# Two projection tiles placed between list products, halved pool clears and an earlier sum of squares, around the first two expert lists of each mixture-of-experts stage

## The chip, the core and the metric

The kernel runs on one core of one Trainium2 chip, as one launch. The metric is device time in microseconds (us), the median of repeated runs of the whole program. All data are 32-bit floats.

## What is computed

One inference step of a decoder with two layers, over 288 tokens (256 of a prompt, 32 of samples) of width 1024. Each layer is a token mixer, then a mixture of experts, then a gated per-layer embedding:

```
for i in range(DEPTH):                       # DEPTH = 2
    hn = _rmsnorm(h, g_mix[i])
    h = h + mixer_i(hn)                      # 0: latent attention, 1: chunked gMLP
    h = h + _hier_moe(_rmsnorm(h, g_ffn[i]), ...)
    h = h + sigmoid(_rmsnorm(h, g_ple[i]) @ w_gate) * (p[i] @ w_proj)
y = _rmsnorm(h, g_final)

def _hier_moe(hn, ...):                      # 32 experts, top 2 of the 8 in the top 1 of 4 groups
    pg = softmax(t @ w_rg + b_rg);  pg_top, g_idx = top_k(pg, 1)
    le_g = (t @ w_re + b_re)[group g_idx];  pe_top, e_idx = top_k(softmax(le_g), 2)
    gates = one_hot(g_idx * 8 + e_idx) * pg_top * pe_top / sum(pe_top)
    a = silu(t @ w_gate) * (t @ w_up) * gates
    return a @ w_down
```

## The kernel before

Tokens lie along the free dimension, features along the 128 partitions, in 8 tiles (KD = 8). All large weights come as one stream of 250 slots of 1 MB through a ring of 12 slots in SBUF. The SP queue issues slot s when slot s - 12 has been released (semaphore `slot_free`): TensorE releases slots with `free_with` on a later matmul, or by a `pe.drain()`. The slots of a layer come in the order in which they are used: one with the projection of the per-layer embedding (`S_PROJ`), 96 with the experts (16 pairs of experts, 6 slots each: four for gate and up, two for down), four for the last gate.

Each engine's program is written out by hand; semaphores tie them together. The change touches the stretch between the last tiles that feed `h` (the output projection of the mixer) and the first expert pair. It runs once per layer, in the function `moe(L)` of each engine:

1. VectorE adds each of the 8 result tiles to `h` (`add_h`, L696), multiplies it by the gain of the norm (`gain`, L700) and adds its squares, which ScalarE made (`sum_sq`, L709). TensorE computes the router's logits of the tile (L1360) and turns the tile into rows of tokens (L1367), both in `route_part`.
2. TensorE sums the squares over the partitions (L1394), ScalarE takes the root (L576), TensorE turns the logits (L1398). ScalarE copies the token rows out of PSUM (L562) and writes them to DRAM (`hn_rows`, L580).
3. VectorE chooses group and experts in a chain of some 30 short instructions (L907 to L929). TensorE meanwhile computes `project(0, 6)`, six of the eight tiles of the embedding's projection (L1411), which ScalarE copies out (L586). ScalarE also computes the exponentials `ex` (L584), which needs a table load.
4. TensorE computes each token's rank in its expert (L1427 to L1432). VectorE builds a 0/1 matrix `member` for a pair of experts (`members`, L954), TensorE multiplies it into a list of token numbers (`list_pair`, L1420), VectorE copies the list out (`take_list`, L962 and L963), and the pool engine gathers the listed rows from DRAM into `x_sel` (`gather`, L352). `x_sel` is cleared before, and so is `y_none`, a block of zeros that is scattered for rows without a token (L341, L342).
5. TensorE turns the gathered rows (`x_turn`, L1448), builds list 3, and begins the first pair: gate and up (L1462), then down (L1471).

Around lists 1 and 2 TensorE runs products of the identity that nothing reads, `keep_busy` (L1151, each one of 128x512): one behind the ranks, one behind `project(6, KD)`, and three behind list 2.

Of the kernel before, what the change touches and what calls it, by code (L numbers as in the profile page):

```python
# [24 lines left out]
D, KD = 1024, 8  # L25
# [59 lines left out]
def program(nc, io, ctx):  # L85
# [251 lines left out]
    def _(pool):  # L337
        def moe(L):

            pool.wait_ge(sem("h_upd"), 8 * (1 if L == 0 else 4))  # L340
            pool.memset(x_sel, 0.0).then_inc(sem("x_clear"), 1)  # L341
            pool.memset(y_none, 0.0).then_inc(sem("x_clear"), 1)  # L342
            pool.wait_ge(sem("hn_rows"), 48 * L + 3 * 16)
            pool.wait_ge(sem("x_clear"), 2 * L + 2)

            def gather(c):

# [55 lines left out]

            for c in range(3):
                gather(c)
            for n in range(PAIRS - 1):
                if n + 3 < PAIRS:
                    gather(n + 3)
                    if n + 3 == PAIRS - 1:
                        scatter_none()  # L410
                scatter(n)
# [44 lines left out]
    def _(act):  # L456
# [97 lines left out]
        def moe(L):  # L554
# [24 lines left out]
            for t, (t0, tn) in enumerate(TOK):  # L579
                act.dma_start(hn_rows[L][t0:t0 + tn, :], hn_tok[0:tn, t, :]).then_inc(sem("hn_rows"), 16)  # L580
            for m in range(KD):
                if m == 5:
                    act.wait_ge(sem("sel"), 2 * L + 2)
                    nc.scalar.activation(ex, dx, ACT.Exp).then_inc(sem("ex"), 1)  # L584
                act.wait_ge(sem("prj_ps"), 8 * L + m + 1)
                nc.scalar.activation(prj[:, m, :], bank(2 + m % 4, T), ACT.Copy).then_inc(sem("prj"), 1)  # L586
# [83 lines left out]
    def _(dve):  # L670
# [213 lines left out]
        for m in range(KD):  # L884
            dve.wait_ge(sem("h_part"), m + 1)
            add_h(m, bank(m % 4, T))
            dve.wait_ge(sem("h_upd"), m + 1)
            gain("ffn0", m, hn_t, G_FFN[0])
            if m >= 1:
                sum_sq("ffn0", m - 1)  # L890
        sum_sq("ffn0", KD - 1)

        io3 = const[:, C_IOTA:C_IOTA + EPG]

# [235 lines left out]
        for m in range(KD):  # L1130
            dve.wait_ge(sem("h_part"), 16 + m + 1)
            add_h(m, bank((m + 1) % 4, T))
            dve.wait_ge(sem("h_upd"), 24 + m + 1)
            gain("ffn1", m, hn_t, G_FFN[1])
            if m >= 1:
                sum_sq("ffn1", m - 1)
        sum_sq("ffn1", KD - 1)
        dve.wait_ge(sem("out"), 64)
        moe(1)
        for k in range(0, KD, 2):  # L1140
# [4 lines left out]
    def _(pe):  # L1145
# [207 lines left out]
            last.then_inc(sem("o_ps"), 1)  # L1353
        owe(1)
        pe.wait_ge(sem("o_sb"), H)
        def route_part(L, k):

            pe.wait_ge(sem("scales"), 2)
            pe.wait_ge(sem("h_upd"), 8 * H_STAGE[f"ffn{L}"] + k + 1)
            last = mm(ps[0:G + NE, 7, 0:T], w_r[:, L, k, :], h_t[:, k, :], start=(k == 0), stop=(k == KD - 1))  # L1360
            if k == KD - 1:
                last.then_inc(sem("lg_ps"), 1)
            pe.wait_ge(sem("h_gain"), 8 * H_STAGE[f"ffn{L}"] + k + 1)
            if k == 4:
                pe.wait_ge(sem("hr_a"), 6 * L + 3)
            for t, (t0, tn) in enumerate(TOK):
                last = nc.tensor.transpose(ps[0:tn, 4 + t, (k % 4) * P:(k % 4) * P + P], hn_t[:, k, t0:t0 + tn], ident)  # L1367
            if k % 4 == 3:
                last.then_inc(sem("hr_ps"), 1)

        for m in range(KD):
            if m % 2 == 0:
                wait_slots(pe, S_O + m // 2, S_O + m // 2 + 1)
            if m >= 4:
                pe.wait_ge(sem("h_upd"), m - 3)
            for k in range(H):
                last = mm(bank(m % 4, T), ring(S_O, m * D + k * P, P), oT[:, k, :], start=(k == 0), stop=(k == H - 1))  # L1377
                if k == 0:
                    free_with(last)
            last.then_inc(sem("h_part"), 1)  # L1380
            if m % 2 == 1:
                owe(1)
            if m >= 2:
                route_part(0, m - 2)

        def moe(L):
            ffn = f"ffn{L}"
            route_part(L, KD - 2)
            route_part(L, KD - 1)

            pe.wait_ge(sem("scales"), 5 + 2 * L)
            pe.wait_ge(sem("h_sum"), 8 * H_STAGE[ffn] + KD)
            for t in range(3):
                last = mm(ps[:, 0, t:t + 1], sq_sum[:, t * P:t * P + P], ones[:, 0:1], start=True, stop=True)  # L1394
            last.then_inc(sem("h_ss"), 1)
            pe.wait_ge(sem("lgs"), L + 1)
            for t in range(3):
                last = nc.tensor.transpose(ps[:, 1, 36 * t:36 * t + 36], lgs[:, t * P:t * P + P], ident[0:G + NE, 0:G + NE])  # L1398
# [33 lines left out]
                last = mm(ps[:, 6, 0:32], ones[0:tn, :], sel[0:tn, t, :], start=(t == 0), stop=(t == 2))  # L1432
            last.then_inc(sem("rank_ps"), 1)
            keep_busy(0, 1)
            project(6, KD)
            keep_busy(0, 1)
            pe.drain().then_inc(sem("slot_free"), 1)

            pe.wait_ge(sem("tv"), 2 * (L + 1))
            list_pair(1, None)  # L1440
            list_pair(2, 1)
            keep_busy(0, 3)
            pe.wait_ge(sem("prj"), 8 * L + KD)

            def x_turn(b):
# [226 lines left out]
        for m in range(KD):  # L1672
            if m >= 4:
                pe.wait_ge(sem("h_upd"), 24 + m - 3)
            last, at = out_part(m, OUT_K if m < 4 else 0, FT, at)
            last.then_inc(sem("h_part"), 1)
            if m >= 2:
                route_part(1, m - 2)
        moe(1)
        sum_norm("fin")  # L1680

# [131 lines left out]
```

## Time and profile before

| | |
|---|---|
| median of 3 runs | 1193.99 us (1192.52 to 1194.03) |
| profiled execution | 1194.44 us |
| its span in the trace | 1192.7 us |
| TensorE busy | 1065.9 us (89%) |
| VectorE, ScalarE, pool busy | 369.3, 189.9, 115.0 us |
| DMA | 306.02 MB, mean 257 GB/s |

In the rows a PE row is TensorE's matmuls (a matmul of 32-bit floats is two records), PEld its weight loads, DVE is VectorE, ACT ScalarE, POOL the pool engine, and SPq, ACTq the sequencers of SP and ScalarE. Times count from the start of the span. PEclk is the clock granted to TensorE as a share of its 2.4 GHz: 1.00 is that level, 0.50 is 1.2 GHz, and a share between them says how much of the stretch was at each.

### The profile page before, as it was taken

How to read it: one execution, taken by the hardware profiler on the slowest of the kernel's cores; microseconds unless marked ns; L12 is line 12 of the kernel's file. 1: busy time of each engine (PE TensorE's matmuls, PEld its weight loads, DVE VectorE, ACT ScalarE, POOL GpSimd, SP SyncE). 2: the span in 40 equal slices, each digit the busy share in tenths (PEclk: the TensorE clock that was granted, in tenths of full speed). 3: DMA queues.
4: the chain of work that ended last, by engine and by line, in shares of the span. 5: the costliest groups of instructions: out<-in, count | busy, mean ns of one | idle time of the engine just before them, and what ended most of it. 6: DMA issues, size and time to landing. Idle time of an engine off the chain costs nothing.

```text
span 1192.7 us, 14363 instructions
## 1 busy us (share of the span) xinstructions
PE 1065.9 (89%) x5248; PEld 656.7 (55%) x5248; DVE 369.3 (31%) x929; ACT 189.9 (16%) x389; POOL 115.0 (10%) x152
## 2 busy tenths in 40 slices
PE   6978699999988886999999999999999998787693
PEld 5747366544433332777777777777644443332272
DVE  4545214322221101562227444221422221110164
ACT  2122112211111101231112110001211111011121
POOL 1333000111111111000000000000111111110101
PEclk9989799899999999999999999999979999999897
DMA  9758282499999996933333323333269999999501
GB/s 367 301 166 257 74 359 108 150 397 421 417 420 419 419 420 256 421 144 138 115 132 141 106 106 106 106 132 138 98 245 411 419 418 418 419 420 382 223 33 40
DMA packets 62613, 306.02 MB, mean 257 GB/s; under 512 B 13746, under 2 KB 23186, under 8 KB 30546
## 3 DMA queue, kind: packets, MB, share of 16 engines
q1 hardware_dynamic: 45936, 275.73, 58.3%
q0 software_dynamic: 13632, 22.58, 5.7%
q10 hardware_dynamic: 2978, 6.80, 1.5%
q8 instruction: 44, 0.72, 0.2%
q14 instruction: 23, 0.19, 0.0%
HBM read 308.10 MB, written 21.08 MB: 276 GB/s over the span
## 4 chain that ended last, share of the span: by engine, by line
PE 64%; DMA 23%; issue 5%; DVE 3%; SPq 3%; ACT 1%; POOL 0%; POOLq 0%; DVEq 0%; ACTq 0%
DMA ring_sb<-stream 23%; PE ps L1607 16%; PE ps L1462 10%; PE ps L1655 8%; PE ps L1471 4%; PE ps L1540 3%; PE ps L1377 3%; PE ps L1160 2%; PE ps L1420 2%; PE ps L1151 2%; PE ps L1202 1%; SPq L292 1%; SPq L293 1%; PE ps L1558 1%; PE ps L1556 1%
## 5 line engine op out<-in xcount | busy, mean ns | idle before, releaser
L1462 PE MATMUL ps<-ring_sb,scr_sb 128*64 128x512 f32 x1024 | 236.4, 609 | 41.0 <-DMA ring_sb<-stream 41.0
L1607 PE MATMUL ps<-hn_sb,ring_sb 128*128 128x288 f32 x768 | 194.9, 408 | 0.0
L1462 PEld LDWEIGHTS ps<-ring_sb,scr_sb 128*64 128x64 f32 x1024 | 78.7, 140 | 194.6 <-issue 194.5
L1607 PEld LDWEIGHTS ps<-hn_sb,ring_sb 128*128 128x128 f32 x768 | 142.6, 190 | 37.3 <-DVE hn_sb L700 0.3
L1471 PE MATMUL ps<-ring_sb,scr_sb 128*64 128x512 f32 x512 | 121.4, 617 | 2.1 <-ACT scr_sb L598 1.9
L986 DVE SCALAR_TENSOR_TENSOR scr_sb<-ps,scr_sb 128x256 f32<-128x256 f32 x32 | 15.5, 483 | 267.0 <-ACT scr_sb L594 267.0
L1655 PE MATMUL ps<-scr_sb,ring_sb 128*128 128x288 f32 x384 | 95.3, 407 | 0.0
L1655 PEld LDWEIGHTS ps<-scr_sb,ring_sb 128*128 128x128 f32 x384 | 72.2, 190 | 19.4
L1471 PEld LDWEIGHTS ps<-ring_sb,scr_sb 128*64 128x64 f32 x512 | 34.9, 141 | 61.7 <-issue 57.4
L1540 PE MATMUL ps<-scr_sb,ring_sb 128*128 128x288 f32 x256 | 64.3, 406 | 0.0
L352 POOL DMA_INDIRECT scr_sb<-hn_rows,scr_sb x32 | 32.4, 1014 | 301.5 <-DVE scr_sb L963 276.7
L1077 DVE TENSOR_TENSOR scr_sb<-ps,rstd_sb 128x288 f32<-128x288 f32 x48 | 21.7, 453 | 124.4 <-PE ps L1607 120.8
L1540 PEld LDWEIGHTS ps<-scr_sb,ring_sb 128*128 128x128 f32 x256 | 48.6, 190 | 13.4
L594 ACT ACTIVATE scr_sb<-ps,scr_sb 128x256 f32<-128x256 f32 x32 | 15.2, 474 | 239.7 <-PE ps L1462 239.7
L991 DVE TENSOR_SCALAR scr_sb<-ps,scr_sb 128x512 f32<-128x512 f32 x32 | 24.0, 751 | 93.0 <-PE ps L1471 89.5
L1420 PEld LDWEIGHTS ps<-tv_sb,scr_sb 128*128 128x128 f32 x384 | 48.2, 202 | 4.6 <-DVE scr_sb L954 2.5
L1420 PE MATMUL ps<-tv_sb,scr_sb 128*128 128x4 f32 x384 | 48.0, 254 | 2.8 <-DVE scr_sb L954 2.4
L696 DVE TENSOR_TENSOR h_sb<-h_sb,ps 128x288 f32<-128x288 f32 x32 | 14.4, 451 | 111.8 <-PE ps L1655 54.0
L341 POOL MEMSET scr_sb<- 128x2048 f32 x2 | 3.6, 1803 | 469.4 <-DVE h_sb L696 469.4
L471 ACT ACTIVATE scr_sb<-h_sb 128x288 f32<-128x288 f32 x48 | 21.1, 439 | 173.5 <-DVE h_sb L696 173.5
L602 ACT ACTIVATE scr_sb<-ps,scr_sb 128x512 f32<-128x512 f32 x32 | 22.0, 687 | 144.5 <-PE ps L1471 140.0
L369 POOL DMA_INDIRECT y_rows<-scr_sb x30 | 29.8, 993 | 144.4 <-DVE scr_sb L991 141.0
(258 smaller groups left out, 1098.6 us busy)
## 6 DMA issues: line engine op xcount, KB each, us to landing
ring_sb<-stream SPq DMA_DIRECT2D x249, 1024.0 KB, 18.3
scr_sb<-key_pages SPq DMA_DIRECT2D x64, 192.0 KB, 3.4
ring_sb<-row_pages POOLq DMA_DIRECT2D x64, 128.0 KB, 3.5
scr_sb<-y_rows POOLq DMA_DIRECT2D x8, 512.0 KB, 5.0
hn_rows<-scr_sb ACTq DMA_DIRECT2D x4, 512.0 KB, 3.1
h_sb<-x SPq DMA_DIRECT2D x1, 1152.0 KB, 5.6
scr_sb<-bs ACTq DMA_DIRECT2D x1, 640.0 KB, 12.9
scr_sb<-p ACTq DMA_DIRECT2D x2, 288.0 KB, 5.2
```

Source lines behind the costliest of these rows:

```text
L352: pool.indirect_dma_start(out=x_sel[:, c % 2, :], out_offset=None, in_=hn_rows[L], in_offset=bass.IndirectOffsetOnAxis(ap=slots[:, c, 0:1] ...
L369: pool.indirect_dma_start(out=y_rows[L], out_offset=bass.IndirectOffsetOnAxis(ap=slots[:, c, 1:2], axis=0), in_=y_sb[:, c % 2, :], in_offs ...
L991: nc.vector.tensor_scalar(y_sb[:, b, 512:1024], bank(6), g[:, 0:1], None, ALU.mult).then_inc(sem(f"y_sb{L}"), 1)
L1151: mm(bank(b), ident, const[:, 0:512], start=True, stop=True)
L1160: last = mm(bank(m, T), ring(S_IN, m * D + k * P, P), hn_t[:, k, :], start=(k == 0), stop=(k == KD - 1))
L1377: last = mm(bank(m % 4, T), ring(S_O, m * D + k * P, P), oT[:, k, :], start=(k == 0), stop=(k == H - 1))
L1420: last = mm(ps[:, 7, 0:4], member[:, q, :], tv[:, q // 3, q % 3, :], start=(q == 0), stop=(q == 5))
L1462: last = mm(ps[64 * a:64 * a + 64, 2 + b, :], xT[:, k, 64 * a:64 * a + 64], slot(a + 2 * (k // 4))[:, (k % 4) * 512:(k % 4) * 512 + 512], ...
L1471: last = mm(ps[64 * a:64 * a + 64, 5 + n, :], aT[:, k, 64 * a:64 * a + 64], slot(4 + k)[:, a * D + n * 512:a * D + n * 512 + 512], start=( ...
L1540: last = mm(bank(PLE_BANK[m % 4], T), ring(s, (m % 2) * D + k * P, P), hgp[:, k, :], start=(k == 0), stop=(k == KD - 1))
L1607: last = mm(bank((i + 1) % 4, T), ring(s, (i % 2) * D + k * P, P), hn_t[:, k, :], start=(k == 0), stop=(k == KD - 1))
L1655: last = mm(bank((m + 1) % 4, T), ring(s, (at % 16) * P, P), uT[:, k, :], start=(k == 0), stop=(k == FT - 1))
```

## The change

In `moe(L)` of TensorE, `route_part` is split into `logits` and `turn_rows`, and the last tile's `turn_rows` goes behind the sum of the squares. On VectorE the last `gain` goes behind the last `sum_sq`. The pool engine clears `x_sel` in two halves, the first when all squares are summed, the second when the first member matrix is there, and `y_none` behind the third gather. ScalarE loads the table of Exp ahead of the fourth projection copy, by a one-column activation. Of the last two projection tiles the seventh goes behind list 1 and the eighth behind list 2; four of the five `keep_busy` products of this stretch are taken out, and the `pe.drain()` that releases the slot of the projection moves behind the eighth tile.

```
             pool.wait_ge(sem("h_upd"), 8 * (1 if L == 0 else 4))        # before
             pool.memset(x_sel, 0.0).then_inc(sem("x_clear"), 1)
             pool.memset(y_none, 0.0).then_inc(sem("x_clear"), 1)
             pool.wait_ge(sem("hn_rows"), 48 * L + 3 * 16)
             pool.wait_ge(sem("x_clear"), 2 * L + 2)
...
             pool.wait_ge(sem("h_sum"), 8 * H_STAGE[f"ffn{L}"] + KD)     # the change
             pool.memset(x_sel[:, 0, :], 0.0).then_inc(sem("x_clear"), 1)
             pool.wait_ge(sem("hn_rows"), 48 * L + 3 * 16)
             pool.wait_ge(sem(f"member{L}"), 2)
             pool.memset(x_sel[:, 1, :], 0.0).then_inc(sem("x_clear"), 1)
             pool.wait_ge(sem("x_clear"), 3 * L + 2)
```

```diff
@@ pool engine, behind the first three gathers
+            pool.memset(y_none, 0.0).then_inc(sem("x_clear"), 1)
+            pool.wait_ge(sem("x_clear"), 3 * L + 3)
@@ ScalarE
             for m in range(KD):
+                if m == 3:
+                    nc.scalar.activation(eps[:, 2:3], eps[:, 0:1], ACT.Exp)
                 if m == 5:
@@ VectorE (the same for ffn1)
-            gain("ffn0", m, hn_t, G_FFN[0])
+            if m < KD - 1:
+                gain("ffn0", m, hn_t, G_FFN[0])
             if m >= 1:
                 sum_sq("ffn0", m - 1)
         sum_sq("ffn0", KD - 1)
+        gain("ffn0", KD - 1, hn_t, G_FFN[0])
@@ TensorE, moe(L)
-            route_part(L, KD - 2)
-            route_part(L, KD - 1)
+            logits(L, KD - 2)
+            turn_rows(L, KD - 2)
+            logits(L, KD - 1)
...
             last.then_inc(sem("h_ss"), 1)
+            turn_rows(L, KD - 1)
             pe.wait_ge(sem("lgs"), L + 1)
...
             keep_busy(0, 1)
-            project(6, KD)
-            keep_busy(0, 1)
-            pe.drain().then_inc(sem("slot_free"), 1)
 
             pe.wait_ge(sem("tv"), 2 * (L + 1))
             list_pair(1, None)
+            project(6, 7)
             list_pair(2, 1)
-            keep_busy(0, 3)
+            project(7, KD)
+            pe.drain().then_inc(sem("slot_free"), 1)
             pe.wait_ge(sem("prj"), 8 * L + KD)
```

TensorE's order behind the ranks of layer 0, before: L1151 is `keep_busy`, L1411 `project`, L1420 `list_pair` (its second stretch of six is list 2), L1448 `x_turn`, L1462 the first pair's gate and up.

```order
L1432 MATMUL ps<-scr_sb,const_sb 128x32 x3
L1151 MATMUL ps<-const_sb 128x512
L1411 MATMUL ps<-scr_sb,ring_sb 128x288 x4
L1151 MATMUL ps<-const_sb 128x512
L1420 MATMUL ps<-tv_sb,scr_sb 128x4 x12
L1151 MATMUL ps<-const_sb 128x512 x3
L1448 MATMUL ps<-const_sb,scr_sb 128x128 x8
L1420 MATMUL ps<-tv_sb,scr_sb 128x4 x6
L1462 MATMUL ps<-ring_sb,scr_sb 64x512 x16
```

The same place in the change, whose lines are L1446 for the ranks, L1160 `keep_busy`, L1434 `list_pair`, L1425 `project`, L1461 `x_turn`, L1475 gate and up:

```order
L1446 MATMUL ps<-scr_sb,const_sb 128x32 x3
L1160 MATMUL ps<-const_sb 128x512
L1434 MATMUL ps<-tv_sb,scr_sb 128x4 x6
L1425 MATMUL ps<-scr_sb,ring_sb 128x288 x2
L1434 MATMUL ps<-tv_sb,scr_sb 128x4 x6
L1425 MATMUL ps<-scr_sb,ring_sb 128x288 x2
L1461 MATMUL ps<-const_sb,scr_sb 128x128 x8
L1434 MATMUL ps<-tv_sb,scr_sb 128x4 x6
L1475 MATMUL ps<-ring_sb,scr_sb 64x512 x16
```

List 1 now stands directly behind one filler product, each list is followed by one tile (two matmuls) of projection, and no filler stands between list 2 and the turn of the gathered rows.

The pool engine's order at the head of its `moe(0)`, before (the semaphores that it waits for in brackets):

```order
L341 MEMSET scr_sb 128x2048 [waits h_upd]
L342 MEMSET scr_sb 128x1024
L352 DMA scr_sb<-hn_rows,scr_sb 128x1024 [waits slots0,hn_rows,x_clear]
L352 DMA scr_sb<-hn_rows,scr_sb 128x1024 [waits slots0]
L352 DMA scr_sb<-hn_rows,scr_sb 128x1024 [waits slots0,x_ps0] x2
```

and in the change (L353 is the gather there):

```order
L341 MEMSET scr_sb 128x1024 [waits h_sum]
L344 MEMSET scr_sb 128x1024 [waits member0,hn_rows]
L353 DMA scr_sb<-hn_rows,scr_sb 128x1024 [waits x_clear,slots0]
L353 DMA scr_sb<-hn_rows,scr_sb 128x1024 [waits slots0]
L353 DMA scr_sb<-hn_rows,scr_sb 128x1024 [waits slots0,x_ps0]
L407 MEMSET scr_sb 128x1024
```

The clear of 2048 columns has become two of 1024 with waits of their own, and the clear of `y_none` stands behind the third gather.

## Rows read from the trace of the kernel before

**Rows 1.** Waits of PE in the expert stage of layer 0 (total, times, longest).

```profile
PE ps L1462 <- DMA ring_sb<-stream: 19.2, 16, 2.3
```

**Rows 2.** Stretches (PE, PEld, DVE, ACT, POOL busy; PEclk, DMA share, GB/s).

```profile
241.00:246.00 5.00, 5.00 (x22) 1.60 (x20) 0.75 (x1) 0.69 (x1) 0.55 (x1) 0.85 0.95 345
251.00:256.00 5.00, 4.79 (x32) 3.08 (x32) 2.37 (x6) 1.45 (x3) 0.52 (x1) 1.00 1.02 418
```

**Rows 3.** The chain in order of time, layer 0 (start, us, what).

```profile
202.92 0.80 PE ps L1394 x6
...
204.03 6.02 PE ps L1411 x24
...
211.71 1.05 PE ps L1151 x2
212.76 1.94 PE ps L1411 x8
...
215.79 1.49 PE ps L1420 x12
...
218.45 2.62 PE ps L1420 x12
221.07 4.90 PE ps L1151 x6
225.98 0.88 PE ps L1448 x8
226.85 1.24 PE ps L1420 x12
228.09 7.04 PE ps L1462 x32
```

**Rows 4.** Timeline of layer 0 (start, us, engine, line, operands, [idle before <-releaser]).

```profile
199.93 1.99 DVE L700 TENSOR_SCALAR hn_sb<-h_sb,par_sb 128x288 f32<-128x288 f32 x1
199.95 1.81 POOL L341 MEMSET scr_sb<- 128x2048 f32 x1 [90.15 <-DVE h_sb L696]
...
201.43 0.68 PE L1360 MATMUL ps<-h_sb,w_r_sb 128*36 128x288 f32 x2
201.69 1.11 POOL L342 MEMSET scr_sb<- 128x1024 f32 x1
...
204.33 0.27 DVE L910 TENSOR_TENSOR scr_sb<-ps,scr_sb 128x108 f32<-128x108 f32 x1
...
209.54 1.28 ACT L584 ACT_TABLE_LOAD   x1
...
211.08 0.17 DVE L935 TENSOR_REDUCE scr_sb<-scr_sb 128x3 f32<-128x12 f32 x1 [0.51 <-ACT scr_sb L584]
...
213.34 0.96 DVE L954 TENSOR_TENSOR scr_sb<-const_sb,scr_sb 128x768 f32<-128x768 f32 x1
...
218.56 1.07 POOL L352 DMA_INDIRECT scr_sb<-hn_rows,scr_sb  x1 [15.75 <-issue]
```

**Rows 5.** Line L700 over the span: durations min/median/max in ns, first and last start.

```profile
L700 DVE TENSOR_SCALAR hn_sb<-h_sb,par_sb x32: 369/370/1994, 167.3 to 1175.1; 128x288 f32<-128x288 f32 x32
```

**Rows 6.** Line L352 in the stretch 218 to 220: its DMA.

```profile
DMA to landing us min/median/max: 3.2/3.2/3.2
```

**Rows 7.** Stretches around the changes of PEclk, columns as in rows 2.

```profile
218.00:219.00 1.00, 0.55 (x3) 0.55 (x4) 0.57 (x2) 0.00 (x0) 0.44 (x1) 0.80 1.00 426
...
225.00:226.00 1.00, 1.00 (x4) 0.37 (x3) 0.00 (x0) 0.00 (x0) 0.00 (x0) 0.79 0.02 4
...
242.00:243.00 1.00, 1.00 (x6) 0.34 (x4) 0.00 (x0) 0.00 (x0) 0.00 (x0) 0.76 0.99 418
...
888.00:891.00 3.00, 3.00 (x8) 0.71 (x6) 0.00 (x0) 0.00 (x0) 0.00 (x0) 0.50 0.68 277
```

**Rows 8.** The chain in order of time: down products of the first pairs.

```profile
239.42 5.12 PE ps L1471 x16
...
885.21 5.31 PE ps L1471 x11
```

More of the change, by code:

```diff
@@ L338, in moe @@
         def moe(L):
-            pool.wait_ge(sem("h_upd"), 8 * (1 if L == 0 else 4))
-            pool.memset(x_sel, 0.0).then_inc(sem("x_clear"), 1)
-            pool.memset(y_none, 0.0).then_inc(sem("x_clear"), 1)
+            pool.wait_ge(sem("h_sum"), 8 * H_STAGE[f"ffn{L}"] + KD)
+            pool.memset(x_sel[:, 0, :], 0.0).then_inc(sem("x_clear"), 1)
             pool.wait_ge(sem("hn_rows"), 48 * L + 3 * 16)
-            pool.wait_ge(sem("x_clear"), 2 * L + 2)
+            pool.wait_ge(sem(f"member{L}"), 2)
+            pool.memset(x_sel[:, 1, :], 0.0).then_inc(sem("x_clear"), 1)
+            pool.wait_ge(sem("x_clear"), 3 * L + 2)
             def gather(c):
@@ L1133, in _ @@
             dve.wait_ge(sem("h_upd"), 24 + m + 1)
-            gain("ffn1", m, hn_t, G_FFN[1])
+            if m < KD - 1:
+                gain("ffn1", m, hn_t, G_FFN[1])
             if m >= 1:
@@ L1137, in _ @@
         sum_sq("ffn1", KD - 1)
+        gain("ffn1", KD - 1, hn_t, G_FFN[1])
         dve.wait_ge(sem("out"), 64)
@@ L1355, in _, with logits @@
         pe.wait_ge(sem("o_sb"), H)
-        def route_part(L, k):
+        def logits(L, k):
             pe.wait_ge(sem("scales"), 2)
@@ L1362, in route_part, with turn_rows @@
                 last.then_inc(sem("lg_ps"), 1)
+        def turn_rows(L, k):
             pe.wait_ge(sem("h_gain"), 8 * H_STAGE[f"ffn{L}"] + k + 1)
@@ L1383, in _ @@
             if m >= 2:
-                route_part(0, m - 2)
+                logits(0, m - 2)
+                turn_rows(0, m - 2)
         def moe(L):
             ffn = f"ffn{L}"
-            route_part(L, KD - 2)
-            route_part(L, KD - 1)
+            logits(L, KD - 2)
+            turn_rows(L, KD - 2)
+            logits(L, KD - 1)
             pe.wait_ge(sem("scales"), 5 + 2 * L)
@@ L1677, in _ @@
             if m >= 2:
-                route_part(1, m - 2)
+                logits(1, m - 2)
+                turn_rows(1, m - 2)
         moe(1)
```

## The prediction

> **What bounds the kernel now.** I read first who waits for whom in the expert stage, then the stretches of that stage, then the chain in order of time ahead of it, then the timeline there with the granted clock. In the expert stage of layer 0 TensorE waits 16 times for the weight stream, 19.2 us in all [rows 1], and from about 251 us the stream moves 418 GB/s with the DMA share at 1.00 [rows 2]. So that stage ends when the stream has brought its last slot. But the stream can only refill what TensorE has released: at 241 to 246 it still moved 345 GB/s [rows 2], because the first pair's slots were coming free too slowly. From there on nothing slackens. A microsecond by which TensorE works off the first pair earlier or later is therefore a microsecond of the stage's end, in each layer; what happens elsewhere inside the stage is not. The mark to watch is the end of the first gate and up product, 228.09 + 7.04 = 235.13 us [rows 3].
>
> Ahead of it the chain is TensorE's [rows 3]: sum of squares, projection, ranks, a filler to 212.76, two projection tiles, a filler, list 1 at 215.79, list 2 at 218.45, three fillers from 221.07, 4.90 us, the turned rows at 225.98, list 3 at 226.85. The fillers are the obvious waste. The first gather was issued at 218.56 [rows 4] and landed 3.2 us later, at 221.8 [rows 6]: the rows lay there for 4.2 us before they were turned.
>
> **The start of the chain.** The last gain took 1.99 us on VectorE beside a clear of 1.81 us on the pool engine [rows 4], where 370 ns is the median of its line [rows 5]: it was held until the clear was done, and both sums of squares behind it with it. With the sums first, they end about 1.9 us sooner. TensorE can't use all of that: it computes the last logits until 201.43 + 0.68 = 202.11 [rows 4], so its sum over partitions starts there and not at 202.92 [rows 3], 0.8 us sooner. Behind it now stands the turn of the last tile (three transposes, 0.5 us by the spacing of that stretch), so the turned logits, and with them VectorE's chain, come about 0.55 us sooner than 204.33 [rows 4]. The first half clear now starts together with the last gain and may hold it for its 1.11 us (a clear of 1024 columns [rows 4]); the gain then ends near 202.2, while TensorE is at the sum: hidden, and 0.5 us at most if it isn't.
>
> The Trainium skill ("SBUF — State Buffer", Who interferes with whom) says that VectorE in its two-port form and the pool engine block each other for a whole instruction, by order of issue. The 1.99 us agree. By it the half clear could also be the one that is held, for 0.4 us, which nobody waits for; the sum is the same.
>
> **The exponentials.** Their table load stood at 209.54 and VectorE waited 0.51 us for them [rows 4]. It now stands ahead of the fourth copy. ScalarE still has its three row writes and five copies to do before the exponentials, so it arrives near 210.05; VectorE, 0.55 us sooner, is there at 209.99 and waits 0.3. That gives 0.2 us more (between 0 and 0.51). The first member matrix, which was done near 213.34 + 0.96 = 214.30 [rows 4], is done at 214.30 - 0.55 - 0.2, some 213.55.
>
> **The lists.** TensorE is through with ranks and one filler 0.3 us sooner, at 212.45, and waits for the matrix. List 1 starts at 213.6, not 215.79: 2.2 us won. It takes 1.49 us [rows 3].
>
> **The clock.** This decides what is left of it. The granted clock was 1.00 until 218.6 (a share of 0.80 in 218 to 219) and 0.50 until 225.4 (0.79 in 225 to 226) [rows 7], that is 1.2 GHz. It fell 3.0 us after the last filler ahead of list 1 ended, with nothing but list 1 and a wait between. In this low stretch list 2 took 2.62 us, where list 3 took 1.24; three fillers took 4.90 us, where one took 1.05 at the high level; the clock came back 4.35 us after these fillers had begun [rows 3, 7]. In the change the unbroken work ends at 212.45 and what follows up to gate and up is lists, waits and two tiles of 0.97 us each (two tiles took 1.94 [rows 3]). I see nothing there that would keep the clock high or bring it back, so I take it as low from somewhere in list 1 until 4.35 us after gate and up has begun. The sum, from 213.6:
>
> - list 1: between 1.49 and 2.62, taken 1.9: to 215.5
> - seventh tile: between 0.97 and 1.94, taken 1.5; it covers VectorE's 1.17 us for the next member matrix (218.45 less 215.79 + 1.49): to 217.0
> - list 2, low: 2.62, to 219.6
> - eighth tile, low: 1.94, to 221.55, and ScalarE's copy with its two handovers, which TensorE waits for, taken 0.6 (no group shows it waited for; the same handovers cost VectorE's list 0.2 to 0.3 and a copy of this size cannot be under the 0.37 of a VectorE gain, so 0.5 to 0.8), to 222.15. The first gather, issued 1.3 us behind list 1's end and landing 3.2 us later, is there by 220 and is not waited for
> - turned rows, low: twice 0.88, to 223.9
> - list 3, low: 2.62, to 226.5
>
> So gate and up begins 1.6 us sooner. But it starts at half clock: of its first 4.35 us half is lost, 2.2 us. It ends at 226.5 + 7.04 + 2.2 = 235.75 against 235.13: 0.6 us later. The fillers' 4.90 us bought the clock, and the change pays for it inside the products that count. The clock fell once more in both layers behind the first gate and up, and I leave that as it is: it is an idle stretch that the change doesn't touch.
>
> **What costs nothing.** The slot of the projection is released near 221.5, not at 215.6: it fetches slot 23, down weights of the second pair, with the ring otherwise full. The cover is the whole first pair; without it, one slot would cost 2.5 us (1.05 MB at 418 GB/s [rows 2]). The second half clear, 1.11 us, runs while TensorE makes list 1 (1.49), and is past before the list is out; if not, the gather comes late by up to 1.1 us and still lands before the eighth tile is copied. The clear of `y_none`, 1.11 us, falls into the first gate and up and may hold VectorE's small operations for row numbers; the product lasts 7 us. SP and ScalarE's DMAs are as many as before; ScalarE's three row writes come 0.5 us sooner.
>
> **The sum.** 0.6 us in each of two layers is 1.2 us. The profiled execution took 1194.44 us, 0.45 over the median of 1193.99; applied to the median, the forecast is 1195.2 us, a change within what can be told from none. Faster or slower by 0.2%, 2.4 us, is what a measurement of this kernel can tell.
>
> **Rivals.**
>
> - Main case, 1193 to 1197.5: chance 0.46.
> - The clock holds all the way. Then only the gather binds: landed at 219.6, turned by 220.5, list 3 by 221.7, where it was 228.09: 6.4 us in each layer, 1181.2 us. Against it: the clock fell with less idling than the change leaves. Chance 0.08.
> - The clock is low for the lists, but the eighth tile and the turned rows, 3.7 us of low-clock work with 0.6 us of waiting in them, bring it back by the start of gate and up. Then the 2.2 us are not lost: 1.6 us won per layer, 1190.8 us. For it: list 2 and three fillers, also work at the low level, did end with the clock back [rows 3, 7]. Chance 0.16.
> - It comes out slower: the clock is low from the start of list 1, which adds 0.7 + 0.4 us to my middle values, and comes back late. In layer 1 the down products that began at 885.21 [rows 8] still ran at 0.50 up to 891 [rows 7], 5.8 us, while in layer 0 those of 239.42 had it back at 242.5, 3.1 us [rows 7, 8]. With 5.8 for 4.35 another 0.7 us is lost: 0.6 + 1.8 = 2.4 us per layer, 1198.8 us. It decides from 1.2 us per layer. Chance 0.20.
> - The change doesn't do what it says, since the stream hides the start of the stage: 1194.0 us. The 345 GB/s [rows 2] speak against it. Chance 0.10.
>
> The Trainium skill ("TensorE: Matmul & The Clock Gate", Part 4) says that transposes don't count like products for the clock. By it the third case falls away, since half of its work is turned rows, and the forecast stays 1195.2; if they did count it would be 1190.8. No row here separates the two, so I keep the chance.
>
> **How the numbers follow.** The range must reach from the third case to the fourth; 1188 leaves room for a shorter low stretch in one layer, 1199 for the long one in both. The case of the held clock, 0.08, is left out, and some 0.05 beyond the upper end. Faster by over 0.2%: 0.08, two thirds of 0.16, and a little of the main case, 0.20. Slower: most of the fourth case and an eighth of the main case, 0.28. The rest, 0.52, is no change.
>
> **What would show it.** List 1 starting 2.2 us sooner, near 213.6; the last gain no longer ahead of the sums; PEclk at 0.50 in the turned rows and for some 4 us of gate and up; gate and up beginning near 226.5 and ending near 235.7. The forecast is wrong if PEclk is 1.00 there, or if the stream at 241 to 246 moves much more or less than 345 GB/s for another reason.

## The result and the profile after

The changed kernel took 1184.86 us (median of 5, 1180.24 to 1185.20), the kernel before beside it 1192.60 us: a ratio of 0.9922, 95% interval 0.9902 to 0.9941, so 0.6 to 1.0% faster. The forecast was 1195.2 in a range of 1188 to 1199. Both the time and the range were wrong. The profiled execution took 1184.96 us, its span is 1183.3 us against 1192.7.

Where the 9.4 us of span lie is read by setting marks of the two traces against each other: the end of the last h update ahead of the expert stage, the start of the first gate and up product, the end of the stage's last down product, and the first product that combines the rows behind it (L1556 before, L1569 after).

| stretch | before | after | difference |
|---|---|---|---|
| start to last h update, layer 0 | 199.89 | 199.18 | -0.7 |
| h update to first gate and up, layer 0 | 28.13 | 26.56 | -1.6 |
| h update to last down product, layer 0 | 268.94 | 268.91 | 0.0 |
| last down product to first combining one, layer 0 ("exit") | 9.84 | 10.68 | +0.8 |
| from there to the last h update, layer 1 | 366.89 | 367.28 | +0.4 |
| h update to first gate and up, layer 1 | 27.92 | 24.18 | -3.7 |
| h update to last down product, layer 1 | 272.69 | 268.59 | -4.1 |
| exit of layer 1 | 11.37 | 5.11 | -6.3 |
| from there to the end | 63.13 | 63.53 | +0.4 |

(All in us; each row on the first gate and up product is part of the row below it.) Layer 0 is much as forecast. Layer 1 isn't, and the largest single difference lies behind the stage, in a stretch that the prediction doesn't mention.

The chain in order of time of the changed kernel, layer 0, which answers to [rows 3] (L917 the start of VectorE's chain, L961 the member matrix, L1434 the lists, L1425 a projection tile, L591 its copy, L1461 turned rows, L1475 gate and up):

```profile
202.94 0.28 DVE scr_sb L917
...
211.36 0.97 DVE scr_sb L961
212.47 1.91 PE ps L1434 x12
214.38 2.13 PE ps L1425 x4
216.50 2.35 PE ps L1434 x12
218.86 2.14 PE ps L1425 x4
221.02 0.42 ACT scr_sb L591
221.49 1.97 PE ps L1461 x8
223.46 2.35 PE ps L1434 x12
225.81 9.34 PE ps L1475 x32
```

and the same view in layer 1:

```profile
859.33 1.49 PE ps L1434 x12
...
861.99 2.72 PE ps L1434 x12
864.70 2.14 PE ps L1425 x4
866.87 0.42 ACT scr_sb L591
867.33 1.73 PE ps L1461 x8
869.07 1.24 PE ps L1434 x12
870.30 7.04 PE ps L1475 x32
```

One kernel, two outcomes. In layer 0 gate and up takes 9.34 us, in layer 1 7.04. The stretches, columns as in [rows 2], say why:

```profile
214.00:230.00 16.00, 15.50 (x52) 10.78 (x54) 7.36 (x24) 1.42 (x3) 4.04 (x4) 0.50 0.46 159
241.00:246.00 5.00, 5.00 (x26) 1.71 (x24) 0.75 (x1) 0.69 (x1) 1.46 (x2) 1.00 1.00 393
862.00:868.50 6.50, 6.00 (x22) 4.89 (x23) 1.65 (x7) 0.74 (x2) 2.02 (x2) 0.50 0.17 39
869.00:877.00 8.00, 8.00 (x45) 3.42 (x43) 4.69 (x14) 0.60 (x1) 1.95 (x2) 1.00 0.83 307
```

In layer 0 the granted clock was 0.50, that is 1.2 GHz, until 230, 4.6 us into gate and up. In layer 1 it was 1.00 from the end of the turned rows on, with no idle-time product behind list 1. The first is the prediction's main case, the second its third rival. The clock also didn't fall a second time in layer 0: at 241 to 246 it was 1.00, and the stream moved 393 GB/s, where the kernel before had 0.85 and 345 GB/s [rows 2].

Now the exit. The chain behind the last down product, kernel before, layer 0 and then layer 1 (L1471 down, L1151 three products of 512 columns that fill time; "issue" is time in which the engine waited for nothing that the profile shows):

```profile
465.18 3.65 PE ps L1471 x16
468.83 5.21 issue
474.04 4.79 PE ps L1151 x6
...
1114.60 3.65 PE ps L1471 x16
1118.25 6.09 issue
1124.35 5.49 PE ps L1151 x6
```

The same of the changed kernel from the end of the down products on (L1160 the fillers):

```profile
468.10 1.48 issue
469.58 0.70 PE ps L1160
470.27 4.28 issue
474.55 4.43 PE ps L1160 x5
...
1114.64 1.24 issue
1115.88 2.41 PE ps L1160 x5
1118.29 0.92 issue
1119.21 0.70 PE ps L1160
```

Between the last down product and these fillers TensorE reads how many tokens the fullest expert has and jumps over the code for further passes. Before, it stood still for 5.21 and 6.09 us there. After, it goes on within 1.24 to 1.48 us, but stops again among the fillers: behind one record of six in layer 0, behind five of six in layer 1. The change touches nothing in this place. A stop that moves by a few instructions when code far ahead is taken out points at the fetching of instructions. The DMA view has a queue for it, and in the stretch of the stop of the kernel before, layer 1 (1114.5 to 1124.3 us), it shows one transfer:

```profile
q8 instruction: 1, 0.02, 0.9%
```

Over the span it is (changed kernel):

```profile
PE 1061.7 (90%) x5232; PEld 656.7 (55%) x5232; DVE 370.4 (31%) x929; ACT 189.9 (16%) x391; POOL 115.0 (10%) x154
q8 instruction: 44, 0.72, 0.2%
```

44 transfers of 16 KB. They come every 10 to 37 us wherever TensorE runs straight on, with one more at each of the two exits. With 5232 records of matmuls that is one transfer for 119 records, or about 60 products of the code.

### The profile page after: what moved, and what is told of

Its sections match the earlier page's. It is cut to its first block, busy times and chain, and to the rows that moved or that the text cites. A ratio compares the mean times of both kernels' runs of the same rounds, so it can differ in the third digit from the quotient of the medians.

```text
span 1183.3 us, 14338 instructions
## 1 busy us (share of the span) xinstructions
PE 1061.7 (90%) x5232; PEld 656.7 (55%) x5232; DVE 370.4 (31%) x929; ACT 189.9 (16%) x391; POOL 115.0 (10%) x154
## 4 chain that ended last, share of the span: by engine, by line
PE 63%; DMA 24%; issue 4%; DVE 4%; SPq 3%; ACT 1%; POOL 0%; POOLq 0%; DVEq 0%; ACTq 0%
DMA ring_sb<-stream 23%; PE ps L1620 16%; PE ps L1475 11%; PE ps L1668 8%; PE ps L1484 4%; PE ps L1553 3%; PE ps L1388 3%; PE ps L1169 2%; PE ps L1434 2%; PE ps L1211 1%; SPq L292 1%; SPq L293 1%; PE ps L1569 1%; PE ps L1571 1%; PE ps L1643 1%
## 5 line engine op out<-in xcount | busy, mean ns | idle before, releaser
L1475 PE MATMUL ps<-ring_sb,scr_sb 128*64 128x512 f32 x1024 | 240.9, 618 | 41.2 <-DMA ring_sb<-stream 41.2
L1475 PEld LDWEIGHTS ps<-ring_sb,scr_sb 128*64 128x64 f32 x1024 | 80.0, 141 | 197.3 <-issue 197.3
L353 POOL DMA_INDIRECT scr_sb<-hn_rows,scr_sb x32 | 32.5, 1014 | 274.8 <-DVE scr_sb L970 251.1
L1553 PEld LDWEIGHTS ps<-scr_sb,ring_sb 128*128 128x128 f32 x256 | 48.6, 190 | 13.4
L1434 PEld LDWEIGHTS ps<-tv_sb,scr_sb 128*128 128x128 f32 x384 | 49.7, 206 | 4.6 <-issue 3.8
L1434 PE MATMUL ps<-tv_sb,scr_sb 128*128 128x4 f32 x384 | 49.0, 257 | 2.3 <-DVE scr_sb L961 2.2
L1461 PEld LDWEIGHTS ps<-const_sb,scr_sb 128*128 128x128 f32 x256 | 28.8, 146 | 27.1 <-issue 24.5
```

What stands on the lines that cost most here:

```text
L353: pool.indirect_dma_start(out=x_sel[:, c % 2, :], out_offset=None, in_=hn_rows[L], in_offset=bass.IndirectOffsetOnAxis(ap=slots[:, c, 0:1] ...
L1434: last = mm(ps[:, 7, 0:4], member[:, q, :], tv[:, q // 3, q % 3, :], start=(q == 0), stop=(q == 5))
L1461: last = nc.tensor.transpose(ps[:, k // 4, (k % 4) * P:(k % 4) * P + P], x_sel[:, b, k * P:(k + 1) * P], ident)
L1475: last = mm(ps[64 * a:64 * a + 64, 2 + b, :], xT[:, k, 64 * a:64 * a + 64], slot(a + 2 * (k // 4))[:, (k % 4) * 512:(k % 4) * 512 + 512], ...
L1553: last = mm(bank(PLE_BANK[m % 4], T), ring(s, (m % 2) * D + k * P, P), hgp[:, k, :], start=(k == 0), stop=(k == KD - 1))
```

## The experiments

"Narrow product" below is this. It moves all code behind it and does little work. It isn't quite free: in layer 0's first pairs, where TensorE hardly waits, two of them for each pair make a pair take 14.04 us and not 13.36 (e6); later the wait for the stream hides them:

```
def one_column(b, n):
    for _ in range(n):
        mm(ps[:, b, 0:1], ident, const[:, 0:1], start=True, stop=True)
```

All results first, from 4 to 12 runs each; exits are read as above from each run's one profiled execution. The kernel before was run along with each group of four: 1193.98, 1194.01, 1194.07 and 1192.85 us.

| run | median us (range) | ratio to before, 95% | exit 0 | exit 1 |
|---|---|---|---|---|
| e1 after, 4 narrow per layer | 1195.93 (1194.2 to 1199.1) | 1.0023 (1.0010, 1.0036) | 9.29 | 9.53 |
| e2 after, 4 of 512 columns per layer | 1193.17 (1190.7 to 1197.9) | 1.0000 (0.9984, 1.0016) | 8.92 | 10.30 |
| e3 before without four fillers | 1187.28 (1184.4 to 1188.7) | 0.9949 (0.9929, 0.9969) | 9.77 | 4.87 |
| e4 before, the four narrowed | 1192.93 (1191.1 to 1196.2) | 0.9996 (0.9982, 1.0010) | 10.03 | 9.63 |
| e5 after, shift by 16 | 1182.00 (1176.0 to 1186.5) | 0.9896 (0.9864, 0.9929) | 5.75 | 3.99 |
| e6 after, shift by 32 | 1180.05 (1178.0 to 1181.2) | 0.9871 (0.9847, 0.9895) | 4.13 | 6.22 |
| e7 after, shift by 48 | 1181.36 (1178.2 to 1185.7) | 0.9870 (0.9840, 0.9899) | 4.16 | 3.89 |
| e8 after, shift by 64 | 1186.26 (1181.3 to 1191.5) | 0.9936 (0.9913, 0.9958) | 8.71 | 5.12 |
| e9 before, shift by 32 | 1183.51 (1182.7 to 1186.0) | 0.9913 (0.9900, 0.9926) | 4.14 | 3.91 |
| e10 lists alone, shift by 32 | 1186.53 (1181.2 to 1190.1) | 0.9932 (0.9911, 0.9954) | 4.14 | 5.93 |
| e11 start alone, shift by 32 | 1180.95 (1178.3 to 1188.7) | 0.9909 (0.9883, 0.9935) | 4.23 | 4.43 |
| e12 as e6 | 1181.43 (1179.9 to 1182.2) | 0.9896 (0.9881, 0.9910) | 4.85 | 4.63 |
| e13 before, no jump | 1183.41 (1181.7 to 1187.3) | 0.9919 (0.9897, 0.9941) | 4.35 | 4.42 |
| e14 after, no jump | 1181.37 (1176.4 to 1185.6) | 0.9886 (0.9857, 0.9915) | 3.73 | 3.54 |
| e15 after, shift by 1 | 1187.09 (1182.6 to 1191.2) | 0.9948 (0.9930, 0.9967) | 8.84 | 5.73 |
| e16 e2, shift by 32 | 1184.10 (1181.1 to 1187.4) | 0.9913 (0.9890, 0.9937) | 4.77 | 3.90 |

**Is it the work or the place of the code? (e1 to e4)** e1 and e2 add to the changed kernel, ahead of the turned rows:

```diff
             pe.drain().then_inc(sem("slot_free"), 1)
+            one_column(0, 4)      # e2: keep_busy(0, 4)
             pe.wait_ge(sem("prj"), 8 * L + KD)
```

e1:

> The changed kernel, with four products of one column per layer where the three idle-time products stood, ahead of the turned rows of the first pair, so that TensorE has as many instructions as in the kernel before, at a cost of some 0.1 us each that the wait for ScalarE's last copy hides. Theory A (the 6 us come from behind the last down product, and depend on where TensorE's instructions lie behind the skipped branch): the time from the last down product to the first combining product goes back to about 9.8 us in layer 0 and 11.4 us in layer 1, 1190 us in all. Theory B (they come from the new order and timing of the lists): it stays at 10.7 and 5.1 us, 1185 us in all.

e2:

> The changed kernel, with four products of 512 columns per layer at that place. Theory A: the exits as in the run with narrow products, and beside that what the products do to the clock and to the first turned rows (up to 1 us a layer either way), 1188 to 1192 us. Theory B, the products cost what the change saved: also about 1190 us, but with exits of 10.7 and 5.1 us and a list stage that is later by 2 to 3 us in each layer.

e3 and e4 leave the kernel before as it is but for its four fillers:

```diff
             project(6, KD)
-            keep_busy(0, 1)
+            # e4: one_column(0, 1)
             pe.drain().then_inc(sem("slot_free"), 1)
...
-            keep_busy(0, 3)
+            # e4: one_column(0, 3)
```

e3:

> The kernel before without four of its five products of 512 columns per layer (the one ahead of the slots' release and the three ahead of the turned rows), all else as it was. Theory A: the exits take about 10.7 and 5.1 us, so 1187 to 1188 us, with the list stages no faster. Theory B: the exits stay at 9.8 and 11.4 us, 1192 to 1195 us.

e4:

> The kernel before with the same four products narrowed to one column. Theory A: exits as in the kernel before, 9.8 and 11.4 us, so 1192 to 1194 us. Theory B: 1192 to 1195 us too. Beside the run without them it shows what the count of instructions is worth where the work is the same.

With eight products of one column more, 16 records, the changed kernel takes 11 us more. Its exits are 9.29 and 9.53 us, 3.0 us longer together. The chain of e1, layer 0:

```profile
470.39 4.94 issue
475.33 4.51 PE ps L1160 x6
```

The stop comes at once, ahead of all six records, as in the kernel before, in e2 and in e4, which have as many products ahead of the jump. Most of the rest of e1's loss is in layer 1's stage, 274.72 us against 268.59: its clock was low to 878, and I come to that below. Part of it is the four products themselves. I had expected 0.1 us each, hidden; at the low clock the four took 1.9 us, and list 3 came 3.6 us behind the eighth tile and not 2.3. The kernel before without four fillers per layer (e3) has exits of 9.77 and 4.87 us, with one record ahead of the stop in layer 0 and five in layer 1, exactly as in the changed kernel, though its lists are the old ones; it gains 6.7 us. Its chain in layer 1 up to the sixth record:

```profile
1118.11 1.27 issue
1119.38 2.41 PE ps L1151 x5
1121.79 0.65 issue
```

With the four narrowed (e4) the gain is gone, 5.7 us in the median and 5.0 us in the exits, which are 10.03 and 9.63 us. Theory A stands; B, that the lists bring the 6 us, fell. The misses: I expected 1190 us for e1, and it took 1195.9, because I left layer 1's clock and the products' own time out of it. For e2 I expected 1188 to 1192, and it took 1193.2. And where the stop comes at once it isn't always as long as the 11.4 us of exit that I expected in layer 1: e1, e2 and e4 had 9.5 to 10.3 there.

**Does it follow the transfers? (e5 to e8)** 1, 2, 3 and 4 narrow products ahead of each of the 16 pairs' gate and up in layer 0:

```diff
                 pe.wait_ge(sem(f"xT{L}"), 2 * (n + 1))
+                one_column(2 + b, 1 if L == 0 else 0)      # 2, 3, 4
                 for k in range(KD):
```

> The changed kernel with one product of one column ahead of each pair's gate and up products in layer 0, 16 in all, about a quarter of the code that one 16 KB transfer of instructions holds (44 transfers for 5232 recorded matmuls, two records to a product, so about 60 products to a transfer). The products lie in stages that wait for the weight stream. Theory C (what matters is where the code behind the skipped branch lies in those transfers): as in the run with four narrow products per layer, the code behind the branch is not there when TensorE jumps, exits of 9 to 10 us in both layers, 1190 to 1196 us. Rival D (any more instructions cost some time everywhere): a little over 1185 us, exits of 10.7 and 5.1 us.

> The same with two such products for each pair of layer 0, 32 in all, about half a transfer. Theory C: either as with a quarter, or, if by now the branch and what lies behind the skipped code are in transfers that follow one another, exits of 4.5 to 5.5 us in both layers and 1179 to 1181 us. Rival D: 1185 to 1187 us, exits of 10.7 and 5.1 us.

> The same with three such products for each pair of layer 0, 48 in all, about three quarters of a transfer. Theory C: the code behind the branch is there when TensorE jumps, with a good part of its transfer left: exits of 4.5 to 5.5 us in both layers, 1179 to 1181 us. Rival D: 1185 to 1188 us.

> The same with four such products for each pair of layer 0, 64 in all, about one whole transfer. Theory C: the place in the transfers is nearly that of the changed kernel, so its exits come back, near 10.7 and 5.1 us or one product to the side of them, 1181 to 1190 us. Rival D: 1186 to 1190 us, and no such swing between the four runs.

More instructions made the kernel faster: 1180 to 1182 us with 16, 32 and 48 of them, and slower again at 64, 1186 us. (At 16 the interval of the ratio still overlaps that of the changed kernel; the exits are short.) With 64 the pattern of the changed kernel is back, one record and then the stop (e8, layer 0):

```profile
469.29 1.45 issue
470.75 0.70 PE ps L1160
471.44 2.33 issue
473.78 4.43 PE ps L1160 x5
```

Rival D fell by this return: a price per instruction rises, it doesn't come back to the same picture after 64 products, about what one transfer holds. What is left of it is the time of the products themselves, as above. For a quarter I had expected the long exits, and it had short ones: the stretch of places in which the code is missing is the narrower part of the period here, not the wider. In the short exits TensorE goes on in one piece (e5, layer 1):

```profile
1106.76 1.31 issue
1108.07 2.84 PE ps L1160 x6
```

and in layer 0 of e5 the combining product then waits another 1.24 us for the rows that the pool engine loads back. That wait is the floor of an exit: the 6.22 us in layer 1 of e6 and the 5.93 us in layer 1 of e10 are it too.

The traces tie the stops to the transfers more closely. In all 16 exits with a stop (both layers of before, after, e1 to e4, e8 and e15) a transfer of 16 KB begins on q8 behind the last down product, and TensorE goes on 1.3 to 1.6 us behind its end, whether the stop is 0.7 or 6.2 us long. The transfer before it lay 21 to 27 us ahead of the end of the last down product. In the 16 exits that have the jump and no stop (e5 to e7, e9 to e12, e16) it lay 0.8 to 19 us ahead, which fits code around the jump that had been fetched more lately.

**How sharp is the border? (e15)** A single narrow product, at the first pair of layer 0.

> The changed kernel with one single product of one column more, in layer 0 ahead of the first pair's gate and up products. Theory A with a sharp border: in layer 0, where one record of an idle-time product ran ahead of the stop, none is left and the stop comes at once, 9 to 10 us of exit; in layer 1, where five records ran ahead of it, three are left and the stop is longer by about their time, 5 to 6 us of exit: 1184 to 1187 us. Rival, no sharp border: exits as in the changed kernel, 10.7 and 5.1 us.

The chain of e15, layer 0 and layer 1:

```profile
467.43 4.46 issue
471.89 4.54 PE ps L1160 x6
...
1112.27 1.28 issue
1113.55 1.55 PE ps L1160 x3
1115.10 1.50 issue
1116.61 1.55 PE ps L1160 x3
```

As expected to the record: one product of two records moved the stop from behind one record to ahead of all, and in layer 1 from behind five to behind three. The exits, 8.84 and 5.73 us, are a little under the 9 to 10 and within the 5 to 6 expected; the median, 1187.09, is just above the 1184 to 1187.

**Is it the jump? (e13, e14)** TensorE's code for further passes left out (these inputs never run it), for a kernel that doesn't jump:

```diff
-            with pe.If(most > WIN):
-                with pe.Fori(PAIRS // 2, PASSES * PAIRS // 2) as i:
...
```

> The kernel before with TensorE's code of the further passes left out (they run only if an expert has more tokens than one window, which these inputs don't have), so that TensorE jumps over nothing; the other engines keep theirs. Theory A, in the form that the jump over code costs a transfer that isn't there: exits of 4 to 6 us in both layers, about 1182 us. Rival, the place in the transfers costs it without a jump too: exits of 8 us or more in one layer at least, 1186 us or more.

> The changed kernel with the same code left out of TensorE's part. Theory A: exits of 4 to 6 us, about 1180 us, and not further from the kernel before without it than 1 to 4 us: the change's own worth once more. Rival as there.

The kernel before goes from 1192.9 to 1183.4 us. Its timeline in layer 1:

```profile
1113.86 2.83 PE L1151 MATMUL ps<-const_sb 128*128 128x512 f32 x6 [0.83 <-issue]
1117.45 0.86 PE L1535 MATMUL ps<-const_sb,scr_sb 128*128 128x128 f32 x6 [0.75 <-DMA scr_sb<-y_rows]
```

and its transfers of instructions:

```profile
q8 instruction: 42, 0.69, 0.2%
```

Two fewer than 44: the ones at the exits are gone, and the wait is for the loaded rows. So both are needed for the stop, the jump and an unlucky place behind it. The Trainium skill says just that ("Runtime: NRT & Kernel Launch", Instruction fetch mechanics): a taken branch whose target isn't among the pages that are held forces a fetch before execution goes on. These runs agree. From the last down product to the first filler it is 4.4 to 6.2 us of "issue" where the code is missing altogether (before, e1, e2, e4, layer 0 of e15), against 1.2 to 1.7 us with a jump to code that is held and 0.8 to 1.1 us without a jump (e13, e14).

**What is the change itself worth? (e9 to e12, e16)** All with 32 narrow products, and no exit in their traces stops. e9 is the kernel before, e10 it with TensorE's list part alone, e11 with the start of the chain alone, e12 the changed kernel again:

```diff
e10, on the kernel before            e11, on the changed kernel
-            project(6, KD)          +            project(6, KD)
-            keep_busy(0, 1)         +            keep_busy(0, 1)
             list_pair(1, None)                   list_pair(1, None)
+            project(6, 7)           -            project(6, 7)
             list_pair(2, 1)                      list_pair(2, 1)
-            keep_busy(0, 3)         +            keep_busy(0, 3)
+            project(7, KD)          -            project(7, KD)
```

> The kernel before with two products of one column for each pair of layer 0, 32 in all, which put the code behind both branches at about the place where the changed kernel with the same 32 found it there. Theory A: exits of 4 to 6 us in both layers instead of 9.8 and 11.4, so 1181 to 1184 us for a kernel with nothing of the change; what the change itself is worth is then what is left against the changed kernel with the same shift (1180 us), 1 to 4 us. Rival: the change's own parts are worth most of the 9 us, then 1186 us or more here.

> The kernel before with TensorE's part around the lists alone (list 1 ahead of the seventh projection tile, the eighth after list 2, four products of 512 columns less), with the same 32 narrow products. Forecast in the prediction's terms: the three idle-time products ahead of the turned rows, 2.6 us at the high or 5 us at the low clock, are gone and the eighth tile, 2.1 us, stands there, so the first gate and up products start 1 to 2 us sooner, of which the weight stream leaves nothing in layer 0 and up to 2 us in layer 1: 0 to 2 us below the kernel before with the same shift.

> The kernel before with the start of the chain alone (last squares summed ahead of the last gain, clears in halves, table of the exponential early, last rows turned later), TensorE's lists as before, with the same 32 narrow products. List 1 is 2 us sooner, by my trace of the changed kernel; if the gate and up products start sooner by as much and the stream is what ends the stage, 0 us in layer 0 and up to 2 us in layer 1: 0 to 2 us below the kernel before with the same shift.

> The changed kernel with the same 32 narrow products once more, on the chip of the three others, so that the four can be set against each other: 1180 us, within 1 us of the first time.

> The changed kernel with four products of 512 columns ahead of the first turned rows and the 32 narrow products. Exits of 4 to 6 us as without the four. If the products pay in clock what they cost: 1180 to 1182 us, as without them. If the clock comes back without them, as it did in layer 1 of the changed kernel: they put the first gate and up products later by up to 2.6 us a layer, and the time is 1182 to 1185 us.

The kernel before with nothing but 32 narrow products takes 1183.5 us: 10.6 us faster, more than the whole change brought. In e9's profiled execution the two exits are 13.2 us shorter together than before and the two stages 4.5 us longer, 2.6 of them in layer 0, where the narrow products stand. The changed kernel with them takes 1181.4, 2.1 us less, and each of its four runs is below each of the other's five; without the jump the two are 2.0 us apart (e13, e14). So the change itself is worth about 2 us, of which the intervals say little more than that it is between 0 and 5. How the two parts share it isn't settled. The lists alone come out at 1186.5 and the start alone at 1181.0, but they range over 9 and 10 us, and the whole is no better than the start. For the lists alone I had expected 0 to 2 us gained, and 3 lost is what the median says; for the start alone 0 to 2 too, and it is 2.6. The changed kernel (e12) came out 1.4 us above its first time (e6), where I had expected it within 1. The four products of 512 columns (e16) gain nothing that shows: 1184.1 against 1181.4, with overlapping intervals, the second of the two cases expected.

**The clock, read across all runs.** This is what made the ranges wide. In every profiled execution the clock fell at the lists or the tile between them, and the low stretch was not of one length. Without fillers behind the lists it was 7 to 17 us long: 17 in layer 0 and 7 in layer 1 of the changed kernel, 17 and 17 in e1, 7 and 7 in e5 and e15, 14 and 14 in e14. With them (before, e2, e9, e11, e13, e16) it was 3 to 10 us. In e5, as in layer 1 of the changed kernel, it was high again before gate and up (columns as in [rows 2]):

```profile
215.00:221.00 6.00, 5.50 (x20) 4.04 (x19) 2.03 (x8) 0.82 (x2) 2.09 (x2) 0.50 0.08 17
222.00:230.00 8.00, 8.00 (x47) 3.85 (x47) 4.68 (x14) 0.60 (x1) 1.95 (x2) 1.00 0.73 283
```

So the same code, with list 1 at 13.3 us behind the last h update to 0.1 us, gets either. What differs is the moment at which the clock fell. The new lists without the four wide products have 17 such stretches in the traces (after, e1, e5 to e8, e14, e15, layer 0 of e12). In nine the clock fell 13.4 to 15.3 us behind the h update, and it stayed low for 14 to 17 us in eight of them; in the other eight it fell later, up to 16.3 us, and it stayed low for 7 us in seven. In the changed kernel that is 14.1 us in layer 0 and 15.8 us in layer 1. Why it falls at one moment and not at another isn't in these traces, and no run sets the moment.

## Why the prediction was wrong, step by step

- **The start of the chain: right.** Forecast 0.55 us sooner for VectorE's chain; it began at 202.94 and not at 204.33 [rows 4], 1.4 us sooner, of which 0.7 are the h update ahead of it that was sooner too, so 0.7 for the forecast 0.55. The last gain took 1.14 us beside a half clear of 0.95, no longer ahead of the sums, and nobody waited for it.
- **The exponentials: right in kind.** The 0.51 us of [rows 4] are gone; 0.2 were forecast.
- **The lists: right.** List 1 forecast at 213.6, measured 212.47, 0.7 us of the difference being the earlier h update, the rest the exponentials (0.3) and the start (0.1). From there to gate and up it took 13.3 us for the forecast 12.9, with 2.1 us instead of 1.5 for the seventh tile as the largest miss.
- **The clock, layer 0: right.** Low from 213.3 until 4.6 us into gate and up, forecast 4.35. Gate and up forecast to begin at 226.5 and end at 235.75; 225.81 and 235.15, on a base 0.7 us sooner, so the end is 0.7 us later than before against the forecast 0.6. Layer 1 shows below that this was one of two outcomes, so there is some luck in it.
- **"A microsecond of the stage's end, in each layer": failed in layer 0, with the wrong mark.** The 0.7 us later end of gate and up changed the stage by 0.0 us (268.94 and 268.91). Across the runs, first gate and up products of layer 0 that begin 24.2 to 24.4 us behind the h update go with stages of 265.1 to 266.3 us (e5, e6, e15), those between 25.0 and 29.3 with 268.1 to 272.7 in no order.
- **"The clock fell once more [...] and I leave that as it is": failed in both layers.** That second low stretch was gone in layer 0 and halved in layer 1. So in layer 0 the first pair's down products ended 43.8 us behind the h update and not 44.7, 0.9 us sooner although gate and up ended later, and the stream at 241 to 246 moved 393 GB/s and not 345, which the prediction names as a sign that it is wrong. The end of the down products is the better mark. In layer 1 of the 18 traces, 40.5 to 40.9 us to that end go with stages of 268.6 to 270.2 us, 42.3 to 44.7 us with 269.3 to 272.7, and 45.4 to 46.3 us with 272.7 to 274.7: there it is near a microsecond for a microsecond.
- **"0.6 us in each of two layers": failed in layer 1.** The third rival came there: turned rows from 867.33, clock back by 868.7, gate and up 3.7 us sooner, the down products behind it 5.35 us instead of 6.56 because the second low stretch was 3.4 us and not 6.8, and the stage 4.1 us shorter. I had given it 0.16 and priced it for both layers together; that the two could differ stands only in the lower end of the range. The Trainium skill's sentence that transposes don't count like products ("TensorE: Matmul & The Clock Gate", Part 4) doesn't rule it out: list 2 and the eighth tile, which are products, ended at 866.8, the turned rows came behind them, and no run here parts the two.
- **"What happens elsewhere inside the stage is not", and no step at all for what lies behind it: the failure that decides.** -6.3 us in layer 1 and +0.8 in layer 0 are 5.4 of the 9.4 us. The 5.2 and 6.1 us of "issue" stood in the chain of the kernel before, with nothing waited for, and I took them as fixed. Where they stop hangs on how many instructions stand ahead of the branch, and the change takes eight products out. e3 shows it with the old lists: 6.7 us from leaving out code.

I gave faster 0.20, and even the 0.16 of the third rival, had it come in both layers, would have been 1190.8. Without the exits, the sum of the differences is -4.0 us, near 1190.

## What to carry to other kernels

Where a kernel jumps over code, its time can hang on where that code lies. Here any edit that added or removed instructions ahead of a skipped block could move the exits behind it by several microseconds, in either direction and whatever it was made for. So look in the chain for "issue" behind a branch and for a transfer of instructions beside it, and compare two versions with a few dozen harmless instructions added to both, or with the block left out, before an edit gets the credit. Here 32 products of one column on the old kernel gained more than the change did, 10.6 us against 7.7, and the two together take 1180 to 1181 us.

A granted clock that came back in one profiled execution is one draw. Two layers with the same code, or a handful of runs, tell what a single stretch can't.

## What the runs showed of the hardware

- From the last product ahead of the jump to the first behind it, TensorE takes 1.2 to 1.7 us where the code behind it is held and stands still for 4.4 to 6.2 us where it isn't (0.8 to 1.1 us where there is no jump, e13 and e14); where part of it is held, that part runs first, and the stop that remains is 0.7 to 4.3 us (after, e3, e8, layer 1 of e15).
- A stop ends 1.3 to 1.6 us behind the end of the transfer of 16 KB, in 16 exits of 16.
- The border is sharp to one product (e15), and the picture returns after 64 products of one column (e8), near the 60 that 44 transfers for 5232 records give.
- With short exits, the combining products begin 3.5 to 6.2 us behind the last down product; where they wait, it is for the rows that are loaded back.
- With the same code, and list 1 at the same time to 0.1 us, the low stretch of TensorE's clock lasted anything from 7 to 17 us, mostly 14 to 17 us where the clock fell within 15.3 us of the h update and 7 us where it fell later.
